# A banded attention with filler products: three Strassen groups in the stage before it, two sets of slots for the turned probabilities, and another order of its steps

## The chip, the cores and the metric

One core of a Trainium2 chip runs the whole kernel in one launch. The metric is the device time of that launch in microseconds (us), as the median of several runs. Engines are named as in the profile: PE is TensorE (PEld its weight load), ACT is ScalarE, DVE is VectorE, POOL is GpSimd, SP is the engine whose queue issues most DMAs.

## What is computed

Two transformer blocks on 1024 tokens of width 1024, all in float32. What matters here is the second block:

```
h = rms_norm(x, norm1_g)
proj = h @ w_in            # 6144 columns: q, k, v (1024 each), bg, cg, xc (1024 each)
q, k = rms_norm per head;  y_attn = chunked_relpos_attention(q, k, v)   # 16 heads of 64
u = cg * xc;  conv = conv_b + sum(conv_w[j] * shifted u);  y_conv = bg * conv
gates = sigmoid(h @ w_gate + b_gate)                                    # 2048 columns
merged = g_attn * (y_attn @ w_attn_proj) + g_conv * (y_conv @ w_conv_proj)
x = x + merged @ w_out;  x = x + square(relu(rms_norm(x) @ w_up)) @ w_down
```

A query of the attention sees the keys of its own chunk of 64 and of the eight chunks before. In tiles of 128 tokens that is a window of at most five key tiles: query tile 0 has one, 1 has two, 2 three, 3 four, and tiles 4 to 7 have five each.

## The kernel before

Every float32 product is made of three matmuls: each operand is split into a high part (rounded to fp32r) and a low part (the rest), and high x high, high x low and low x high are summed in PSUM. Splitting costs ACT or POOL (high) and POOL or DVE (low).

**The stage before the attention** (`phase_qkv`) computes q, k and v, with two "units" of Strassen products (7 products for 8), and then `BCX_GROUPS` more Strassen groups, each for 512 of the 3072 columns bg, cg, xc. A group is 7 products of 24 matmuls (168), where the plain way takes 192. The rest of the 3072 columns, and 7 of the 8 chunks of `w_gate`, are left to be computed as plain "chunks" of 256 columns: a chunk is 4 filler products of 8 steps in k, each step 3 matmuls of 128x512. Only in the last group is the operand of product m6 restored from a copy in DRAM (`spare_x`, loaded by SP at L1897 behind the stores of q and k, L1850; ACT L2091 makes the high part), and the weights of the last product are split behind that on ACT (L2010) and POOL (L1923).

**The attention** (`phase_attention`) goes through 8 pairs of heads, 16 steps a pair, 8 a head; step n of a pair belongs to query tile n % 8. In step n the engines do, in this order (block counts are those of the tile meant):

- PE: half of the step's filler (`product_part`, here 6 matmuls); at odd n the values of the tile pair n-3, n-2 (`values`, L2379, 4 to 12 matmuls); the transposes of the probabilities of tile n-1 (`turn`, L2366); the other half of the filler; the scores of tile n+2 (`scores`, L2354); at n % 8 = 1 and 4 four transposes of raw q and k of the next head (`round_`, L2391). The scores of tile n+2 wait until DVE has read those of tile n+1 (semaphore `shifted`); the turns of tile n-1 wait for its scaled probabilities and for `lo_p`, the low parts of tile n-2.
- ACT: the exponentials of tile n+1 (`exps`, L2517); the eviction of a filler product (`product_out`, L2482) or its store; the high parts of tile n-1 (`high`, L2533); at odd n half of the values' output (`o_tmp`, L2555); at n % 8 = 2 and 5 the high parts of the next head's q and k (`round_hi`, L2466 and L2469, three instructions); v at n % 8 = 3, DMAs at 0 and 7.
- DVE: the bias and the row maximum of tile n+1 (`largest`, L2628); reciprocal and scaling of tile n (L2655, L2656); the low parts of tile n-1 (`low`, L2647); at odd n the sum of the values (L2665); at n % 8 = 3 and 6 the low parts of the next head's q and k (`round_lo`, L2596 and twice L2599); v at 5.
- POOL splits one chunk of filler weights per head (L159, L164); SP loads it.

Every engine works through its list in order; semaphores alone tie the lists. Pairs 1 to 6 run in a hardware loop on PE, ACT and DVE; the first and the last are written out. The high and low parts of turned tiles stand in one set of six slots, so `high` of the next tile pair waits for the values of the one before it.

Of the kernel before, what the change touches and what calls it, by code (L numbers as in the profile page):

```python
# [13 lines left out]
P = 128  # L14
# [40 lines left out]
def program(nc, io, out):  # L55
    ctx = ExitStack()
    with ctx:
# [47 lines left out]
        BCX_GROUPS = 1  # L105
# [2145 lines left out]
        def phase_attention(pairs, src, q_col, k_col, v_col, back, ext, norm_gains, w_start, dst, banks_read, ready_first, ready_rest):  # L2251
# [11 lines left out]
            TAIL = 2 * (STEPS + 2)  # L2263

            def tail_step(x):
                return next(n for n in range(STEPS + 2) if 8 * KB * (2 * n + 2) // TAIL >= KB * (x + 1))
            S_BANK, PT_BANK, O_BANK, G_BANK, T_BANK = 0, 2, 4, 5, 7
            with ExitStack() as mem:
# [9 lines left out]
                pt_hi = sb(mem, "pt_hi_2", [P, nslot, 256], F32R)  # L2278
                pt_lo = sb(mem, "pt_lo_2", [P, nslot, 256], F32R)
# [26 lines left out]
                feed(block, w_start, 2 * pairs + 1, lambda j: (mm_h, j * 4 + 4))  # L2306
# [5 lines left out]
                def pair_loop(eng, body):  # L2312


                    body(0, True, False)
                    with eng.Fori(0, pairs - 2) as j:
                        body(j + 1, False, False)
                    body(pairs - 1, False, True)
# [11 lines left out]
                def pt_groups(m):  # L2330

                    k0, k1 = window(m % 8)
                    sl = k0 - (2 * ((m % 8) // 2) - back)
# [12 lines left out]
                def _(pe):  # L2346
# [23 lines left out]
                    def values(i, m):  # L2370
                        h, g = m % STEPS // 8, (m % 8) // 2
                        pe.wait_ge(lo_p, i * STEPS + (m + 2))

                        pe.wait_ge(o_done, i * 8 + (m // 2 + 1))
                        first, last_kb = window(2 * g)[0], window(2 * g + 1)[1] - 1
                        for kb in range(first, last_kb + 1):
                            sl = kb - (2 * g - back)
# [17 lines left out]
                    def product(chunk, x, ks, out_index):  # L2395
# [3 lines left out]
                        if 0 in ks:  # L2399
                            if x % 4 == 0:  # L2400
                                pe.wait_ge(split_done, chunk + 1)
                            if isinstance(out_index, int) and out_index < 2:
# [13 lines left out]
                    def product_part(i, n, h, last):  # L2416

                        part = 2 * n + h
                        ends = (8 * KB * part // TAIL, 8 * KB * (part + 1) // TAIL) if last else (2 * part, 2 * part + 2)
                        for x in range(ends[0] // KB, (ends[1] - 1) // KB + 1):  # L2420
                            ks = range(max(ends[0] - x * KB, 0), min(ends[1] - x * KB, KB))
                            product(i * 2 + (w_start + 1 + x // 4), x, ks, i * 8 + (EARLY + x))
# [24 lines left out]
                    pair_loop(pe, body)  # L2447

                @block.scalar
                def _(act):  # L2450
# [27 lines left out]
                    def product_out(i, x):  # L2478

                        act.wait_ge(mm_h, i * 8 + (EARLY + x + 1))  # L2480
                        act.wait_ge(st_h[x % 2], (i * 4 + (EARLY + x) // 2 + 1) * 16)
                        nc.scalar.activation(stage[:, x % 2, :], ps[:, G_BANK + x % 2, :], ACT.Copy).then_inc(ev_h, 1)  # L2482

                    def product_store(i, x):

                        act.wait_ge(ev_h, i * 8 + (EARLY + x + 1))
                        act.dma_start(dst[bass.ds(i * (4 * P) + (EARLY + x) // 2 * P, P), (x % 2) * 512:(x % 2 + 1) * 512],
                                      stage[:, x % 2, :]).then_inc(st_h[x % 2], 16)
# [9 lines left out]
                    for r in range(2):  # L2498
                        product_out(0, r - EARLY)
                        product_store(0, r - EARLY)  # L2500
# [4 lines left out]
                    product_out(0, 2 - EARLY)  # L2505
                    product_store(0, 2 - EARLY)
# [14 lines left out]

                    def body(i, first, last):
                        for n in range(STEPS + 2 if last else STEPS):
                            hh, nn = n // 8, n % 8
                            prepare = n < STEPS and not (last and n >= 8)
                            def high():
                                if n <= STEPS and not (first and n < 1):
# [3 lines left out]
                                    act.wait_ge(valued, i * 8 + (m // 2 + 1))  # L2531
# [5 lines left out]

                            if n + 1 < STEPS or not last:
                                exps(i, n + 1)
                            if last and n >= 2:  # L2540
                                for x in range(8):
                                    if n == tail_step(x) + 2:
                                        product_store(i, x)
                                    if n == tail_step(x) + 1:
                                        product_out(i, x)
                            elif n % 2 == 0:
                                product_out(i, n // 2 - 1)
                            else:
                                product_store(i, n // 2 - 1)
                            high()  # L2550
                            if n % 2 and not (first and n < 2):
                                m = n - 2
                                act.wait_ge(valued, i * 8 + (m // 2 + 2))
                                act.wait_ge(o_done, i * 8 + (m // 2 + 1))
                                nc.scalar.activation(o_tmp[:, :], ps[HD:P, O_BANK, 0:256], ACT.Copy).then_inc(o_half, 1)  # L2555
# [14 lines left out]
                    pair_loop(act, body)  # L2570
                    for x in range(8):
                        if tail_step(x) + 1 >= STEPS + 2:
                            product_out(pairs - 1, x)
                        if tail_step(x) + 2 >= STEPS + 2:
                            product_store(pairs - 1, x)

                @block.vector
                def _(dve):
# [5 lines left out]
                    for pt in (pt_hi, pt_lo):  # L2584
                        nc.vector.memset(pt[:, nslot - 1, 0:P].bitcast(F32), 0.0)
                        nc.vector.memset(pt[:, 0, P:256].bitcast(F32), 0.0)
# [47 lines left out]

                    def body(i, first, last):
                        link = Chain(dve, dve_self, i * PER)
                        for n in range(STEPS + 2 if last else STEPS):
# [21 lines left out]
                            if n % 2 and not (first and n < 2):  # L2659
                                m = n - 2  # L2660
                                h, g = m % STEPS // 8, (m % 8) // 2
                                dve.wait_ge(o_half, i * 8 + (m // 2 + 1))
                                pair = i + (m // STEPS)
                                out_rows = res[h * HD:(h + 1) * HD, bass.ds(pair, 1), g * 256:(g + 1) * 256]
                                nc.vector.tensor_tensor(out_rows.rearrange("p a n -> p (a n)"), ps[0:HD, O_BANK, 0:256],  # L2665
                                                        o_tmp[:, :], ALU.add).then_inc(o_done, 1)
# [8 lines left out]
                    pair_loop(dve, body)  # L2675

            products = 8 * pairs + EARLY
            return ([(st_h[s], 16 * (4 * pairs + EARLY // 2 + 1)) for s in range(2)],
# [905 lines left out]
        with nc.Block() as block:  # L3584
# [5 lines left out]
            feat_stored, banks_read = phase_attention(8, qkv2, 0, 1024, 2048, 4, ext2, (io["q_norm_g_2"], io["k_norm_g_2"]), W_BCX2, feat2[512 * BCX_GROUPS:, :],  # L3590
                            banks_read, ready_first, ready_rest)
            opened, banks_read = phase_merge(W_GATE + 5 + 2 * BCX_GROUPS, feat_stored, banks_read)
# [78 lines left out]
```

## Time and profile before

| | us |
|---|---|
| median of 3 runs (2171.71 to 2173.11) | 2171.82 |
| the profiled execution | 2173.93 |
| its span, first to last instruction | 2172.1 |
| PE busy in it | 2145.6 |
| DVE, POOL, ACT busy | 1472.0, 998.3, 949.6 |
| attention steps in it, about | 698 to 1256 |

A matmul's end is modelled in these records, and records overlap; what one costs in a stream is the distance to the next start. Mean granted TensorE clock is 0.998.

### The profile page before, as it was taken

The numbers are of one execution on the slowest core, as the hardware profiler recorded it, in microseconds if no ns is written. First come the engines' busy times: TensorE is split into PE (matmuls) and PEld (weight loads), VectorE is DVE, ScalarE is ACT, GpSimd is POOL, SyncE is SP. The second block draws the span as 40 slices with busy tenths as digits, with TensorE's granted clock in tenths as the row PEclk, the third lists the DMA queues.
The fourth block names the chain that finished last, engine by engine and source line by source line (L and its number), as shares of the span: only waits on it lengthen the run. The fifth ranks groups of instructions, "written<-read, shape, count | busy, mean of one in ns | idle before, by whom it ended". The sixth has DMA issues, their size and how long they took to land.

```text
span 2172.1 us, 29103 instructions
## 1 busy us (share of the span) xinstructions
PE 2145.6 (99%) x10450; PEld 1788.2 (82%) x10450; DVE 1472.0 (68%) x2585; ACT 949.6 (44%) x1696; POOL 998.3 (46%) x701
## 2 busy tenths in 40 slices
PE   8999999999998999999999999999999999999999
PEld 8888888888887888888888888788878887888887
DVE  7776775265874666666666658543776777898886
ACT  5555425343342555555555531212555454433332
POOL 3232465454644131322223147457466565556564
PEclk9999999999999999999999999999999999999999
DMA  7320124332226332323333256315143545826433
GB/s 231 105 76 21 45 91 152 126 117 97 87 88 176 89 108 69 112 72 104 88 93 88 69 195 241 107 49 194 49 154 140 171 146 185 319 93 228 150 122 115
DMA packets 198606, 269.34 MB, mean 124 GB/s; under 512 B 58136, under 2 KB 116280, under 8 KB 198368
## 3 DMA queue, kind: packets, MB, share of 16 engines
q1 hardware_dynamic: 124880, 201.38, 27.5%
q10 hardware_dynamic: 73616, 66.49, 10.0%
q8 instruction: 68, 1.11, 0.2%
q14 instruction: 42, 0.34, 0.1%
HBM read 191.23 MB, written 85.00 MB: 127 GB/s over the span
## 4 chain that ended last, share of the span: by engine, by line
PE 76%; DVE 9%; ACT 5%; DMA 4%; issue 4%; POOL 1%; ACTq 1%; DVEq 0%; SPq 0%; POOLq 0%
PE ps L204 64%; PE ps L2379 3%; DMA w_raw<-in_w_up_dram 2%; PE ps L2354 2%; PE ps L2366 2%; DVE res L3476 1%; DVE mlp_acc L3476 1%; PE ps L776 1%; DMA u_parts<-res 1%; PE ps L751 1%; PE ps L762 1%; DVE k_lo L2599 1%; ACT w_hi L3323 1%; DVE a_lo L446 1%; DVE mlp_acc L3464 1%
## 5 line engine op out<-in xcount | busy, mean ns | idle before, releaser
L204 PE MATMUL ps<-a_hi,w_hi 128*128 128x512 f32 x1376 | 536.9, 407 | 7.4 <-DVE res L2149 5.1
L159 POOL TENSOR_TENSOR w_hi<-w_raw,zero 128x512 fp32r<-128x512 f32 x172 | 203.5, 1214 | 735.6 <-PE ps L204 604.9
L204 PE MATMUL ps<-a_hi,w_lo 128*128 128x512 f32 x1376 | 516.6, 392 | 0.0
L204 PE MATMUL ps<-a_lo,w_hi 128*128 128x512 f32 x1376 | 514.0, 390 | 0.0
L204 PE MATMUL ps<-w_hi,a_hi 128*128 128x512 f32 (+1 forms) x960 | 368.5, 384 | 4.1 <-POOL w_lo L672 2.2
L204 PE MATMUL ps<-w_hi,a_lo 128*128 128x512 f32 (+1 forms) x960 | 367.1, 382 | 0.0
L204 PE MATMUL ps<-w_lo,a_hi 128*128 128x512 f32 (+1 forms) x960 | 366.8, 382 | 0.0
L204 PEld LDWEIGHTS ps<-a_hi,w_lo 128*128 128x128 f32 x1376 | 258.4, 188 | 57.7
L204 PEld LDWEIGHTS ps<-a_hi,w_hi 128*128 128x128 f32 x1376 | 258.8, 188 | 50.8 <-POOL w_lo L1923 5.5
L204 PEld LDWEIGHTS ps<-a_lo,w_hi 128*128 128x128 f32 x1376 | 259.8, 189 | 40.8
L164 POOL TENSOR_TENSOR w_lo<-w_raw,w_hi 128x512 fp32r<-128x512 f32 x172 | 243.4, 1446 | 3.4
L204 PEld LDWEIGHTS ps<-w_hi,a_hi 128*128 128x128 f32 x960 | 180.4, 188 | 40.7 <-POOL w_lo L672 2.4
L204 PEld LDWEIGHTS ps<-w_hi,a_lo 128*128 128x128 f32 x960 | 180.4, 188 | 35.5
L204 PEld LDWEIGHTS ps<-w_lo,a_hi 128*128 128x128 f32 x960 | 180.4, 188 | 35.2
L2647 DVE TENSOR_TENSOR pt_lo<-ps,pt_hi 128x512 fp32r<-128x512 f32 (+1 forms) x192 | 88.3, 488 | 149.0 <-ACT pt_hi L2533 149.0
L2517 ACT ACTIVATE prob<-prob,st 128x640 f32<-128x640 f32 (+4 forms) x128 | 89.4, 698 | 224.5 <-DVE st L2628 223.5
L3237 POOL TENSOR_TENSOR w_lo<-mlp_raw_b,w_hi 128x512 fp32r<-128x512 f32 x60 | 99.0, 1678 | 56.5 <-ACT w_hi L3323 56.5
L3257 POOL TENSOR_TENSOR w_lo<-mlp_raw_more,w_hi 128x512 fp32r<-128x512 f32 x56 | 89.5, 1630 | 62.2 <-ACT w_hi L3354 62.2
L3481 DVE TENSOR_TENSOR a_lo<-mlp_part,a_hi 128x512 fp32r<-128x512 f32 x104 | 108.8, 1094 | 4.8 <-ACT a_hi L3363 4.8
L2628 DVE CUSTOM_DVE_ANT_0 prob<-ps,bias 128x640 f32<-128x640 f32 (+4 forms) x128 | 83.7, 654 | 23.6 <-issue 22.8
L3237 POOL TENSOR_TENSOR w_lo<-w_raw,w_hi 128x512 fp32r<-128x512 f32 x44 | 66.0, 1528 | 63.9 <-ACT w_hi L3323 63.9
L1923 POOL TENSOR_TENSOR w_lo<-qkv_raw,w_hi 128x512 fp32r<-128x512 f32 x46 | 67.2, 1494 | 58.5 <-ACT w_hi L2010 58.5
(307 smaller groups left out, 3929.9 us busy)
## 6 DMA issues: line engine op xcount, KB each, us to landing
mlp_part<-u_parts SPq DMA_DIRECT2D x26, 1024.0 KB, 7.9
w_raw<-in_w_in_dram SPq DMA_DIRECT2D x24, 1024.0 KB, 5.3
feat_fm<-stage ACTq DMA_DIRECT2D x68, 256.0 KB, 2.1
u_parts<-mlp_acc SPq DMA_DIRECT2D x28, 512.0 KB, 2.8
u_parts<-res SPq DMA_DIRECT2D x28, 512.0 KB, 2.8
conv_in<-feat_fm ACTq DMA_DIRECT2D x24, 512.0 KB, 5.5
res<-in_x_dram SPq DMA_DIRECT2D x16, 512.0 KB, 6.4
w_raw<-in_w_out_dram SPq DMA_DIRECT2D x8, 1024.0 KB, 5.1
```

Of the source, the lines that this page charges most:

```text
L159: hi = nc.gpsimd.tensor_tensor(w_hi[slot][:, k:k + 2, :], w_raw[:, k:k + 2, :], zero[:, 0:1].unsqueeze(2).to_broadcast([P, 2, CW]), ALU.add)
L164: lo = nc.gpsimd.tensor_tensor(w_lo[slot][:, k:k + 2, :], w_raw[:, k:k + 2, :], w_hi[slot][:, k:k + 2, :].bitcast(F32), ALU.subtract)
L204: last = nc.tensor.matmul(out_of(o), lhs, rhs(o), start=first and n == 0, stop=final and n == 2)
L1923: ins = nc.gpsimd.tensor_tensor(weight(w_lo, s)[:, at, :], raw_weight(s)[:, at, :], weight(w_hi, s)[:, at, :].bitcast(F32), ALU.subtract)
L2354: last = nc.tensor.matmul(ps[:, S_BANK + bank, 0:c1 - c0], q_st[:, head_slot, b * P:(b + 1) * P], kk[:, head_slot, k0 * P + c0:k0 * P + c1 ...
L2379: last = nc.tensor.matmul(ps[:, O_BANK, 0:256], v_st[:, h, kb, :], pt[:, sl, :], start=(kb == first and pt is pt_hi), stop=(kb == last_kb ...
L2517: nc.scalar.activation(prob[:, s, 0:w], prob[:, s, 0:w], ACT.Exp, scale=-1.0, bias=st[:, s, 1:2], accum_out=st[:, s, 2:3]).then_inc(exped, 1)
L2628: nc.vector.tensor_tensor_reduce(out=tile_view(prob, s, 0, nk), in0=score_view(nk), in1=tile_view(bias, hh, off, nk), scale=-1.0, scalar=3 ...
L2647: ins = nc.vector.tensor_tensor(pt_lo[:, sl:sl + cnt, cols], ps[:, bank, 0:cnt * P].rearrange("p (j n) -> p j n", n=P), pt_hi[:, sl:sl + c ...
L3237: ins = nc.gpsimd.tensor_tensor(low[:, k:k + 2, :], up_raw(p)[:, k:k + 2, :], high[:, k:k + 2, :].bitcast(F32), ALU.subtract)
L3257: ins = nc.gpsimd.tensor_tensor(down_slot(w_lo, s)[:, k, :], raw_of[p][h][:, k, :], down_slot(w_hi, s)[:, k, :].bitcast(F32), ALU.subtract)
L3481: nc.vector.tensor_tensor(down_operand(a_lo, s)[:, k, :], staged(s)[:, k, :], down_operand(a_hi, s)[:, k, :].bitcast(F32), ALU.subtract).t ...
```

## The change

`BCX_GROUPS` goes from 1 to 3, so two more Strassen groups run before the attention and four chunks fewer are filler: 13 instead of 17. The filler is spread evenly over all 130 steps. The loops over pairs are written out. `pt_hi` and `pt_lo` get two sets of slots. On PE the turns come ahead of the second part of the filler and the values last; on ACT `high` comes first, then at even n the half of the values, then `exps`; DVE sums the values at even n, a step later.

```diff
-        BCX_GROUPS = 1
+        BCX_GROUPS = 3
+        FILL_CHUNKS = 13
...
-            TAIL = 2 * (STEPS + 2)
+            FILLED = 4 * (fill_chunks - 1)
+            PARTS = 2 * (STEPS * pairs + 2)
+            def filled_to(part):
+                return FILLED * KB * part // PARTS
+            def last_step(x):
+                return next(n for n in range(PARTS // 2) if filled_to(2 * n + 2) >= KB * (x + 1))
+            OUT_AT = {0: -1, **{last_step(x) + 1: x for x in range(FILLED)}}
+            STORE_AT = {n + 1: x for n, x in OUT_AT.items()}
...
-                pt_hi = sb(mem, "pt_hi_2", [P, nslot, 256], F32R)
-                pt_lo = sb(mem, "pt_lo_2", [P, nslot, 256], F32R)
+                pt_hi = sb(mem, "pt_hi_2", [P, 2 * nslot, 256], F32R)
+                pt_lo = sb(mem, "pt_lo_2", [P, 2 * nslot, 256], F32R)
...
-                feed(block, w_start, 2 * pairs + 1, lambda j: (mm_h, j * 4 + 4))
+                feed(block, w_start, fill_chunks, lambda j: (mm_h, j * 4 + 4))
...
+                    for i in range(pairs):
+                        body(i, i == 0, i == pairs - 1)
...
# PE
-                            product_part(i, n, 0, last)
+                            product_part(i, n, 0)
                             if first and n == 0:
                                 scores(0, 1, 0)
-                            if n % 2 and not (first and n < 2):
-                                values(i, n - 2)
                             if n <= STEPS and not (first and n < 1):
                                 turn(i, n - 1)
-                            product_part(i, n, 1, last)
+                            product_part(i, n, 1)
                             if n + 2 < STEPS or not last:
                                 ...
                                 scores(i, n + 2, (n + 2) // 8 % 2)
+                            if n % 2 and not (first and n < 2):
+                                values(i, n - 2)
# ACT
-                                    act.wait_ge(valued, i * 8 + (m // 2 + 1))
+                                    if i * 8 + m // 2 > 1:
+                                        act.wait_ge(valued, i * 8 + m // 2)
...
+                            high()
+                            if n % 2 == 0 and not (first and n < 4):
+                                out_half(i, n - 3)
                             if n + 1 < STEPS or not last:
                                 exps(i, n + 1)
-                            (store or eviction of a product, by the parity of n)
-                            high()
-                            if n % 2 and not (first and n < 2):
-                                (half of the values of tiles n-3, n-2)
+                            step = STEPS * i + n
+                            if step in STORE_AT:
+                                product_store(STORE_AT[step])
+                            if step in OUT_AT:
+                                product_out(OUT_AT[step])
# DVE
                             low()
-                            if n % 2 and not (first and n < 2):
-                                (sum of the values of tiles n-3, n-2)
+                            if n % 2 == 0 and not (first and n < 4):
+                                out_sum(i, n - 3)
```

## Rows read from the trace of the kernel before

**Rows 1.** The page: busy time, share and instructions of each engine.
```profile
PE 2145.6 (99%) x10450; PEld 1788.2 (82%) x10450; DVE 1472.0 (68%) x2585; ACT 949.6 (44%) x1696; POOL 998.3 (46%) x701
```

**Rows 2.** Waits of PE, 560 to 700 us (us, times, longest).
```profile
PE ps L204 <- DVE res L2149: 5.1, 1, 5.1
```

**Rows 3.** Timeline: start us, length us, engine, line, operation, [idle before <-releaser]; ACT.
```profile
662.22 1.91 ACT L2091 ACTIVATE a_hi<-qkv_spare 128x2048 fp32r<-128x2048 f32 x1 [9.53 <-DMA qkv_spare<-spare_x]
```

**Rows 4.** Timeline of PE behind that wait.
```profile
668.14 0.63 PE L204 MATMUL ps<-a_lo,w_hi 128*128 128x512 f32 x1
...
668.57 0.63 PE L204 MATMUL ps<-a_hi,w_lo 128*128 128x512 f32 x1
```

**Rows 5.** The chain of work: the same values one pair of heads on.
```profile
867.03 1.49 PE ps L2379 x12
...
936.92 1.50 PE ps L2379 x12
```

**Rows 6.** Timeline of PE, attention: steps 3 and 4 of a head.
```profile
1044.91 0.27 PE L2354 MATMUL ps<-k_hi,q_st 128*128 128x256 f32 x1
...
1045.14 0.40 PE L204 MATMUL ps<-a_hi,w_hi 128*128 128x512 f32 x1
...
1059.40 0.28 PE L2379 MATMUL ps<-pt_hi,v_st 128*128 128x256 f32 x1
...
1059.87 0.49 PE L2366 MATMUL ps<-ident,prob 128*128 128x128 f32 x3
...
1061.58 0.45 PE L2354 MATMUL ps<-k_hi,q_st 128*128 128x320 f32 x2
...
1062.16 0.39 PE L204 MATMUL ps<-a_hi,w_hi 128*128 128x512 f32 x1
...
1063.55 0.60 PE L2366 MATMUL ps<-ident,prob 128*128 128x128 f32 x4
...
1065.38 0.45 PE L2354 MATMUL ps<-k_hi,q_st 128*128 128x320 f32 x2
```

**Rows 7.** Timeline of DVE, the same steps and two others.
```profile
1043.83 0.29 DVE L2628 CUSTOM_DVE_ANT_0 prob<-ps,bias 128x128 f32<-128x128 f32 x1
...
1060.99 0.56 DVE L2647 TENSOR_TENSOR pt_lo<-ps,pt_hi 128x384 fp32r<-128x384 f32 x1 [1.35 <-ACT pt_hi L2533]
...
1061.51 0.42 DVE L2665 TENSOR_TENSOR res<-ps,o_tmp 64x256 f32 x1
...
1061.96 0.74 DVE L2596 SCALAR_TENSOR_TENSOR q_st<-ps,gains,q_st 64x512 fp32r<-64x512 f32 x1
...
1064.38 0.82 DVE L2628 CUSTOM_DVE_ANT_0 prob<-ps,bias 128x640 f32<-128x640 f32 x1
...
1070.81 0.89 DVE L2647 TENSOR_TENSOR pt_lo<-ps,pt_hi 128x512 fp32r<-128x512 f32 x2 [1.39 <-ACT pt_hi L2533]
```

**Rows 8.** Timeline of ACT, steps 2, 3 and 5 of a head.
```profile
1054.94 0.73 ACT L2517 ACTIVATE prob<-prob,st 128x512 f32<-128x512 f32 x1 [1.83 <-DVE st L2628]
...
1055.78 0.60 ACT L2482 ACTIVATE stage<-ps 128x512 f32<-128x512 f32 x1
...
1056.28 0.38 ACT L2533 ACTIVATE pt_hi<-ps 128x256 fp32r<-128x256 f32 x1
...
1056.54 0.68 ACT L2466 ACTIVATE q_st<-ps,gains 64x512 fp32r<-64x512 f32 x1
...
1057.23 1.38 ACT L2469 ACTIVATE k_hi<-ps,gains 64x512 fp32r<-64x512 f32 x2
...
1060.47 0.49 ACT L2533 ACTIVATE pt_hi<-ps 128x384 fp32r<-128x384 f32 x1 [0.47 <-PE ps L2366]
...
1070.01 0.77 ACT L2533 ACTIVATE pt_hi<-ps 128x512 fp32r<-128x512 f32 x2 [0.30 <-PE ps L2366]
```

**Rows 9.** Groups of DVE by shape, attention: busy us, mean ns | idle.
```profile
L2656 DVE TENSOR_SCALAR prob<-prob,st 128x640 f32<-128x640 f32 x64 | 35.4, 554 | 2.3
...
L2656 DVE TENSOR_SCALAR prob<-prob,st 128x256 f32<-128x256 f32 x16 | 17.9, 1116 | 0.6
```

More of the change, by code:

```diff
@@ L2249, in phase_qkv, with phase_attention @@
                     [store_q[0, 1].at(32), store_q[1, 1].at(32), b_store[0].at(16 * NG), b_store[1].at(16 * NG)])
-        def phase_attention(pairs, src, q_col, k_col, v_col, back, ext, norm_gains, w_start, dst, banks_read, ready_first, ready_rest):
+        def phase_attention(pairs, src, q_col, k_col, v_col, back, ext, norm_gains, w_start, fill_chunks, dst, banks_read, ready_first, ready_rest):
             nslot = back + 2
@@ L2262, in phase_attention @@
             EARLY = 4
-            TAIL = 2 * (STEPS + 2)
-            def tail_step(x):
-                return next(n for n in range(STEPS + 2) if 8 * KB * (2 * n + 2) // TAIL >= KB * (x + 1))
+            FILLED = 4 * (fill_chunks - 1)
[6 more added lines that the diff above has]
+            STORE_AT = {n + 1: x for n, x in OUT_AT.items()}
+            assert len(OUT_AT) == FILLED + 1
             S_BANK, PT_BANK, O_BANK, G_BANK, T_BANK = 0, 2, 4, 5, 7
@@ L2310, in window, with pair_loop @@
                     return max(0, b - back), b + 1
[L2312 to L2318, printed above, removed]
+                def pair_loop(body):
+                    for i in range(pairs):
+                        body(i, i == 0, i == pairs - 1)
                 def pieces(nk):
@@ L2332, in pt_groups @@
                     k0, k1 = window(m % 8)
-                    sl = k0 - (2 * ((m % 8) // 2) - back)
+                    sl = k0 - (2 * ((m % 8) // 2) - back) + nslot * (m // 2 % 2)
                     cols = slice((m % 2) * P, (m % 2 + 1) * P)
@@ L2376, in values @@
                         for kb in range(first, last_kb + 1):
-                            sl = kb - (2 * g - back)
+                            sl = kb - (2 * g - back) + nslot * (m // 2 % 2)
                             for pt in (pt_hi, pt_lo):
@@ L2401, in product @@
                                 pe.wait_ge(split_done, chunk + 1)
-                            if isinstance(out_index, int) and out_index < 2:
+                            if out_index < 2:
                                 pe.wait_ge(*banks_read[out_index])
@@ L2414, in product, with product_part @@
                             last.then_inc(mm_h, 1)
[L2416 to L2422, printed above, removed]
+                    def product_part(i, n, h):
+                        part = 2 * (STEPS * i + n) + h
+                        begin, end = filled_to(part), filled_to(part + 1)
+                        for x in range(begin // KB, (end + KB - 1) // KB):
+                            ks = range(max(begin - x * KB, 0), min(end - x * KB, KB))
+                            product(w_start + 1 + x // 4, x, ks, EARLY + x)
                     for x in range(EARLY):
@@ L2444, in body @@
                                 scores(i, n + 2, (n + 2) // 8 % 2)
+                            if n % 2 and not (first and n < 2):
+                                values(i, n - 2)
                             if n % 8 in (1, 4) and not (last and n >= 8):
                                 round_(i * 2 + (n // 8 + 1), n % 8 // 4)
[L2447 removed]
+                    pair_loop(body)
                 @block.scalar
@@ L2475, in v_high, with product_out, product_store @@
                         nc.scalar.activation(v_st[:, slot, :, 0:HD], v_raw[:, :, :], ACT.Copy).then_inc(hi_v, 1)
-                    def product_out(i, x):
-                        act.wait_ge(mm_h, i * 8 + (EARLY + x + 1))
-                        act.wait_ge(st_h[x % 2], (i * 4 + (EARLY + x) // 2 + 1) * 16)
+                    def product_out(x):
+                        act.wait_ge(mm_h, EARLY + x + 1)
+                        act.wait_ge(st_h[x % 2], ((EARLY + x) // 2 + 1) * 16)
                         nc.scalar.activation(stage[:, x % 2, :], ps[:, G_BANK + x % 2, :], ACT.Copy).then_inc(ev_h, 1)
[L2484 to L2488, printed above, removed]
+                    def product_store(x):
+                        act.wait_ge(ev_h, EARLY + x + 1)
+                        row = (EARLY + x) // 2 * P
+                        act.dma_start(dst[row:row + P, (x % 2) * 512:(x % 2 + 1) * 512], stage[:, x % 2, :]).then_inc(st_h[x % 2], 16)
                     for ready in ready_first:
@@ L2498, in _ @@
                     for r in range(2):
-                        product_out(0, r - EARLY)
-                        product_store(0, r - EARLY)
+                        product_out(r - EARLY)
+                        product_store(r - EARLY)
                         if r == 0:
@@ L2504, in _ @@
                     nc.scalar.activation(st[:, 3, 3:4], zero[:, 0:1], ACT.Exp)
-                    product_out(0, 2 - EARLY)
-                    product_store(0, 2 - EARLY)
+                    product_out(2 - EARLY)
+                    product_store(2 - EARLY)
                     act.wait_ge(lo_r, 3)
@@ L2520, in _, with out_half @@
                     exps(0, 0)
+                    def out_half(i, m):
+                        act.wait_ge(valued, i * 8 + (m // 2 + 2))
+                        act.wait_ge(o_done, i * 8 + (m // 2 + 1))
+                        nc.scalar.activation(o_tmp[:, :], ps[HD:P, O_BANK, 0:256], ACT.Copy).then_inc(o_half, 1)
                     def body(i, first, last):
@@ L2536, in high @@
                                     ins.then_inc(hi_p, 1)
+                            high()
+                            if n % 2 == 0 and not (first and n < 4):
+                                out_half(i, n - 3)
                             if n + 1 < STEPS or not last:
                                 exps(i, n + 1)
[L2540 to L2549, printed above, removed]
-                            high()
-                            if n % 2 and not (first and n < 2):
[L2552 to L2555, printed above, removed]
+                            step = STEPS * i + n
[3 more added lines that the diff above has]
+                                product_out(OUT_AT[step])
                             if prepare:
@@ L2569, in body @@
                                     load_head(i * 2 + (hh + 2))
[L2570 to L2575, printed above, removed]
+                    pair_loop(body)
+                    out_half(pairs - 1, STEPS - 1)
+                    for x in range(FILLED):
+                        if last_step(x) + 1 >= PARTS // 2:
+                            product_out(x)
+                        if last_step(x) + 2 >= PARTS // 2:
+                            product_store(x)
                 @block.vector
@@ L2584, in _ @@
                     for pt in (pt_hi, pt_lo):
-                        nc.vector.memset(pt[:, nslot - 1, 0:P].bitcast(F32), 0.0)
-                        nc.vector.memset(pt[:, 0, P:256].bitcast(F32), 0.0)
+                        for side in range(2):
+                            nc.vector.memset(pt[:, nslot * side + nslot - 1, 0:P].bitcast(F32), 0.0)
+                            nc.vector.memset(pt[:, nslot * side, P:256].bitcast(F32), 0.0)
                     nc.vector.memset(bias[0:HD, :, wmax - HD:wmax], NEG)
@@ L2633, in _, with out_sum @@
                     largest(0, 0, True)
+                    def out_sum(i, m):
+                        h, g = m % STEPS // 8, (m % 8) // 2
+                        dve.wait_ge(o_half, i * 8 + (m // 2 + 1))
+                        pair = i + (m // STEPS)
+                        out_rows = res[h * HD:(h + 1) * HD, bass.ds(pair, 1), g * 256:(g + 1) * 256]
+                        nc.vector.tensor_tensor(out_rows.rearrange("p a n -> p (a n)"), ps[0:HD, O_BANK, 0:256],
+                                                o_tmp[:, :], ALU.add).then_inc(o_done, 1)
                     def body(i, first, last):
@@ L2658, in body @@
                             low()
-                            if n % 2 and not (first and n < 2):
[L2660 to L2666, printed above, removed]
+                            if n % 2 == 0 and not (first and n < 4):
+                                out_sum(i, n - 3)
                             if n < STEPS and not (last and n >= 8):
@@ L2674, in body @@
                             link.close(PER)
-                    pair_loop(dve, body)
-            products = 8 * pairs + EARLY
-            return ([(st_h[s], 16 * (4 * pairs + EARLY // 2 + 1)) for s in range(2)],
+                    pair_loop(body)
+                    out_sum(pairs - 1, STEPS - 1)
+            products = FILLED + EARLY
+            return ([(st_h[s], 16 * (products // 2 + 1)) for s in range(2)],
                     [[(o_done, 8 * pairs + 1), (ev_h, products - 1)], [(ev_h, products), (lo_r, 4 * pairs + 1)],
```

4 lines of the change are left out of this document (2 added, 2 removed).

## The prediction, made before the changed kernel was run

> **What bounds the kernel now.** I read the page first: PE is busy for 2145.6 of 2172 us [rows 1], so whatever takes matmuls out of its list, or a pause out of it, is worth its full time, and whatever makes it wait costs its full time. The waits view of the stage before the attention has one large pause: 5.1 us, once, in the Strassen group [rows 2]. ACT's timeline names its source: 9.53 us of idle time in front of the high parts of the restored operand, ended by the DMA of `spare_x` [rows 3]; the weights of the last product are split behind it. The matmuls after the pause stand 0.43 us apart [rows 4], those elsewhere 1.39/6 = 0.232 us (rows 6: 1062.16 to 1063.55 is one half of a step's filler).
>
> In the attention the timelines show PE without a gap worth the name, so there its list is the time. One pair of heads takes 936.92 - 867.03 = 69.89 us [rows 5]. What PE itself needs comes from distances of starts [rows 6]: half of the filler (six matmuls) 1.39; transposes of 3 blocks and half a filler 1.71, so 0.32 for 3 blocks, 1.83 - 1.39 = 0.44 for 4, hence 0.56 for 5 and 0.20 for 2; scores of 5 blocks 0.58, of few blocks 0.23; values 0.47 for 4 matmuls. A pair is 32 x 1.39 + 72 values matmuls (8.5) + transposes of two heads (2 x 3.3) + four `round_` (1.8) + scores (7.1) = 68.5. So 1.4 us of a pair are small waits and the loop.
>
> What matters more is how close the other engines are. DVE starts the maximum of tile 5 at 1064.38 and takes 0.82 [rows 7]; the scores of tile 6, which wait for it, start at 1065.38 [rows 6]. That is the release with no slack: PE arrives at just the time at which DVE is done. The chain behind this is (tiles counted from 1): transposes of tile 3 on PE, their high parts on ACT, low parts on DVE, then `round_lo`, 2.42 us from its start to the next maximum (1061.96 to 1064.38), then the maximum, then the scores. Filler on PE is the only thing that covers it.
>
> **The change part by part.**
>
> *Matmuls.* 17 chunks become 13: 4 x 4 x 24 = 384 matmuls go from the attention, 384 x 0.232 = 89.1 us. Two groups of 168 come before it: 336 x 0.232 = 77.9. Net -11.2. DVE, ACT and POOL work of a group (one product takes PE 24 x 0.232 = 5.6 us) fitted in the existing group but for the one pause, so I cost it at nothing; if each added group had a pause like that one, it would be +6.3 each, the upper end.
>
> *The pause of the restored operand.* SP issues the load of `spare_x` behind the stores of q and k, before it turns to the groups, in both kernels; it is needed in the last group. With two groups of 38.9 us in front, a DMA that came 9.5 us late is there long before. I take the whole pause off: 5.1 us and the slow matmuls behind it, six at +0.2: -6.3. The other end is 0, if another release stands right behind; the weights of that product are then split two products ahead, so I see none. The added loads of SP (four of 1 MB, two stored results more) are issued a group ahead of use.
>
> *Old small waits of the attention.* They come from ACT doing the exponentials, which wait for DVE, before the high parts. `high` now goes first, and the second set of slots lets it pass the values. 1.4 x 8 = -11; the other end is 0. Written-out steps instead of a loop: their cost lies within the same 1.4 a pair downward, and as much upward, since other written-out stages run six matmuls in the same 1.39; I take 0. The four added memsets stand in DVE's wait at the start of the stage. ACT has 16 stores and evictions fewer, SP and POOL four chunks fewer: nothing on PE's path.
>
> *Less cover, two places in a head.* A step had 12 filler matmuls; now it has 1152/130 = 8.9, so a half is 1.03 us instead of 1.39. DVE's and ACT's lists are as long as before.
>
> First place, scores of the next head's second tile, in step 7. From the start of the transposes of the sixth tile PE passes: transposes 0.56, half, scores 0.23, half, transposes 0.56, half = 4.43 us (the values, which stood in between, are now behind these scores; before it was 3 x 1.39 + 1.35 + 1.43 for twelve values matmuls = 6.95). The chain that the scores wait for: transposes to high parts 0.60 for 3 blocks (1059.87 to 1060.47), 0.84 for 5; to low parts 0.80 (1070.01 to 1070.81 [rows 7, 8]); low parts 0.89; the sum of the values 0.45, which now falls in just this step, an even one; `round_lo` 2.42; the maximum of one block to the scores 1.00 - (0.82 - 0.29) = 0.47 [rows 7]. Sum 5.87. So PE waits 1.44 us. Before, without the sum, it was 5.42 against 6.95: hidden.
>
> Second place, the scores of the seventh tile, in step 4. PE passes from the transposes of tile 3: 0.32, half, scores 0.58, values 0.47, half, 0.44, half = 4.90. The chain: 0.60 + 0.52 + 0.52 (1060.47, 1060.99, 1061.51) + 2.42 + 1.00 = 5.06, a wait of 0.16. But ACT is late too: it now does, in step 2, the high parts of two blocks (0.26), the half of the values (about 0.4, by DVE's sum of the same tile), the exponentials (0.84), in 37 of 100 steps an eviction (0.50), and `round_hi` (0.69 + 1.38 = 2.07) *after* the transposes of that step, where before the exponentials and the eviction came ahead of them [rows 8]. From the start of those transposes it is free for the next high parts after 0.48 + 0.26 + 0.40 + 0.84 + 2.07 = 4.05, or 4.55; they are ready after 0.20 + 1.03 + 0.58 + 1.03 + 0.60 = 3.44. Late by 0.61 or 1.11, mean 0.80. The wait is 0.96.
>
> Together 2.4 us in each of the 15 heads that prepare a next one: +36. What is behind a PE that waits is all its filler, so none of it comes back. Ends: 0, if the lists slide apart somewhere that I don't see; 15 x 3.4 = +51, if an eviction and a blocked scaling (below) fall in every time.
>
> *Sum* against the profiled execution (2173.93; span 2172.1): -11.2 - 6.3 - 11 + 36 = +7.5, 2181.4. The median of before lies 2.1 under that execution, so 2179 to be compared with 2171.82; I say 2180.
>
> **A rule that speaks against the change.** Scaling 256 columns takes DVE 1116 ns on average, 640 columns only 554 [rows 9]: POOL splits its chunk in the first steps of each head, where the small tiles are, and blocks it there. The Trainium skill ("SBUF — State Buffer", "Who interferes with whom") says that `tensor_scalar` in its two-port mode and GpSimd exclude each other for a whole instruction; this trace agrees, by those two means.
>
> **Rivals.**
>
> 1. *The waits are hidden; PE stays the bound.* Then the time is -28.5: 2143. For it: PE is the bound nearly everywhere now, and DVE has work for two thirds of the time. Against it: the release with no slack at step 4 [rows 6, 7]. It decides if the chain of 5.87 us is shorter by 1.4.
> 2. *Only the place in step 7 waits.* ACT's list is in time after all, so step 4 costs 0.16: 15 x 1.6 = 24, sum -4.5, 2167. For it: ACT is the least loaded. Against: the order of its list.
> 3. *Slower by more, by blocked scalings.* There are 13 splits in 130 steps instead of one at each head's start, so they drift onto five-block tiles, where DVE is the chain. A hit costs up to 1.1 - 0.35 = 0.75 us; one that counts per head is 15 x 0.75 = +11 on the forecast: +19, 2191. It decides once scalings of 640 columns average above 0.75 us. Against it: the scaling stands in front of low parts that are not ready for about 1 us.
> 4. *The added groups bring their own pause* each, +12.6 on the forecast, 2192. Against: what caused the pause is in the last group only.
>
> **Chances.** Forecast (-4 to +17 around +7.5) 0.45, rival 1 0.13, rival 2 0.20, rival 3 0.14, rival 4 0.08. About 0.2% (4.3 us) can be told from no change. Faster by more: rival 1, half of rival 2, a little of the forecast's low end: 0.28. Slower: most of the forecast, rivals 3 and 4: 0.50. Between: 0.22. The likeliest case alone is 2168 to 2189; the range, to hold 8 in 10, is 2151 to 2196.
>
> **What would show it.** In the trace after: scores (L2354) waiting for DVE's maximum (L2628) about 30 times, at some 1 and 1.4 us; a pair of heads in 69.9 - 12 + 5 - 1.4, about 61.5 us, against 56.9 under rival 1; no wait at L2149 or for `qkv_spare`; each added group 38.9 us; DVE's wait for the high parts much smaller. Wrong if a pair takes under 58.5 us: then the two places don't wait; or if PE waits elsewhere, at the transposes or values, for more than 10 us in all.

## The result and the profile after

Six runs of the changed kernel have a median of 2182.36 us (2179.49 to 2183.69), against 2172.26 for the kernel before: ratio 1.0044, 95% interval 1.0033 to 1.0055. It is slower by 10 us; 2180 was forecast, with a range of 2151 to 2196. Lines have moved by 1 to 16 in the changed file: the scores are L2362 (before L2354), the transposes L2374, the values L2387, the transposes of raw q and k L2399, DVE's maximum L2636, `round_lo` L2604 and L2607, the low parts L2663.

The page of the profile after: its span, PE's row, and the first of the chain's shares by line.

```profile
span 2181.6 us, 28219 instructions
...
PE 2134.2 (98%) x10402; PEld 1778.7 (82%) x10402; DVE 1505.6 (69%) x2619; ACT 959.3 (44%) x1714; POOL 1009.5 (46%) x697
...
PE ps L205 73%; PE ps L2387 3%; DVE k_lo L2607 2%; PE ps L2362 2%; PE ps L2374 1%; PE ps L777 1%; DVE q_st L2604 1%; PE ps L752 1%; PE ps L763 1%; DVE prob L2636 1%; DVE pt_lo L2663 1%; DMA v_raw<-qkv_tm 1%; PE ps L2399 1%; DVE a_lo L447 1%; ACT k_hi L2477 1%
```

PE is busy 11.4 us less than in [rows 1], in a span 9.5 us longer. Where that is, the windows view shows, cut at the end of the last Strassen stage and at the end of the last values of the attention (columns: stretch, its length, busy us and instructions of PE, PEld, DVE, ACT, POOL, then clock, DMA share, GB/s). Before:

```profile
628.50:677.60 49.10, 44.04 (x187) 35.85 (x187) 35.53 (x41) 14.54 (x19) 19.65 (x15) 0.97 0.33 113
677.60:1255.80 578.20, 574.92 (x3182) 485.43 (x3182) 369.22 (x1014) 308.47 (x693) 154.63 (x136) 1.00 0.33 93
1255.80:2172.10 916.30, 906.98 (x4006) 746.57 (x4004) 660.16 (x663) 348.96 (x441) 534.15 (x344) 1.00 0.45 157
```

After:

```profile
628.50:748.00 119.50, 119.50 (x525) 98.27 (x524) 65.95 (x72) 36.26 (x54) 59.17 (x43) 1.00 0.32 109
748.00:1268.40 520.40, 490.12 (x2803) 415.25 (x2802) 361.21 (x1017) 295.58 (x677) 122.13 (x104) 1.00 0.32 88
1268.40:2181.60 913.20, 904.83 (x4000) 744.55 (x4000) 671.62 (x663) 350.08 (x441) 538.26 (x344) 1.00 0.45 158
```

The first stretch, from the same start, is 70.4 us longer, the attention 57.8 shorter, the rest 3.1 shorter. In the first stretch the 5 us without PE are gone and the clock is 1.00: two added groups cost 70.4, which is 336 matmuls (77.9) less a pause of some 7.5. `spare_x` is now loaded at 653.38, and ACT's use of it comes at 729.63 without a wait where [rows 3] had 9.53 us:

```profile
653.38 0.51 SPq L1898 DMA_DIRECT2D qkv_spare<-spare_x  x1
```

```profile
729.63 1.90 ACT L2092 ACTIVATE a_hi<-qkv_spare 128x2048 fp32r<-128x2048 f32 x1
```

The waits of PE in the attention (us, times, longest):

```profile
PE ps L2362 <- DVE st L2636: 25.5, 27, 1.3
...
PE ps L2399 <- DMA v_raw<-qkv_tm: 3.4, 2, 2.4
...
PE ps L2374 <- DVE prob L2672: 0.5, 1, 0.5
...
PE ps L2374 <- DVE pt_lo L2663: 0.2, 1, 0.2
```

The first row is the forecast one; the same view of the kernel before has it once, with 0.6 us. The view counts idle time only from the modelled end of the matmul before; measured by the distance of starts less the usual distance (waits above 0.15 us counted), the waits in front of the scores are 30 and sum to 30.8 us, 0.28 to 1.48 each, at two tiles of each head that prepares a next one. Here is one of step 7, three engines:

```profile
852.20 0.71 PE L2374 MATMUL ps<-ident,prob 128*128 128x128 f32 x5
...
856.07 0.40 PE L205 MATMUL ps<-a_hi,w_lo 128*128 128x512 f32 x1
...
857.77 0.38 PE L2362 MATMUL ps<-k_hi,q_st 128*128 128x256 f32 x1 [1.30 <-DVE st L2636]
```

```profile
852.95 0.77 ACT L2547 ACTIVATE pt_hi<-ps 128x512 fp32r<-128x512 f32 x2 [0.64 <-PE ps L2374]
```

```profile
851.97 1.38 DVE L2672 TENSOR_SCALAR prob<-prob,st 128x640 f32<-128x640 f32 x1
853.75 0.89 DVE L2663 TENSOR_TENSOR pt_lo<-ps,pt_hi 128x512 fp32r<-128x512 f32 x2 [0.40 <-ACT pt_hi L2547]
...
854.55 0.41 DVE L2648 TENSOR_TENSOR res<-ps,o_tmp 64x256 f32<-64x256 f32 x1
...
854.99 0.74 DVE L2604 SCALAR_TENSOR_TENSOR q_st<-ps,gains,q_st 64x512 fp32r<-64x512 f32 x1
...
855.75 1.53 DVE L2607 SCALAR_TENSOR_TENSOR k_lo<-ps,gains,k_hi 64x512 fp32r<-64x512 f32 x2
...
857.41 0.29 DVE L2636 CUSTOM_DVE_ANT_0 prob<-ps,bias 128x128 f32<-128x128 f32 x1
```

The transposes of the sixth tile start at 852.20. High parts at 852.95, low parts at 853.75, the sum of the values at 854.55, `round_lo` at 854.99, the maximum at 857.41, the scores at 857.77: the chain is 5.57 us. PE was through with its own list at 856.07 + 0.23 = 856.30, which is 4.10 us after the same transposes, so it waited 1.47. The next pairs of heads:

```profile
931.22 1.44 PE ps L2387 x12
...
992.71 1.42 PE ps L2387 x12
...
1115.07 1.44 PE ps L2387 x12
...
1177.45 1.42 PE ps L2387 x12
```

61.5 and 62.4 us, where [rows 5] had 69.9. All seven such distances lie between 60.7 and 65.9 us, with a mean of 62.3.

### The profile page after: what moved, and what is told of

Same layout as the page of the kernel before. It is cut to its first block, busy times and chain, and to the rows that moved or that the text cites. A ratio compares the mean times of both kernels' runs of the same rounds, so it can differ in the third digit from the quotient of the medians.

```text
span 2181.6 us, 28219 instructions
## 1 busy us (share of the span) xinstructions
PE 2134.2 (98%) x10402; PEld 1778.7 (82%) x10402; DVE 1505.6 (69%) x2619; ACT 959.3 (44%) x1714; POOL 1009.5 (46%) x697
## 4 chain that ended last, share of the span: by engine, by line
PE 83%; DVE 7%; ACT 4%; issue 2%; DMA 2%; POOL 1%; ACTq 0%; DVEq 0%; SPq 0%; POOLq 0%
PE ps L205 73%; PE ps L2387 3%; DVE k_lo L2607 2%; PE ps L2362 2%; PE ps L2374 1%; PE ps L777 1%; DVE q_st L2604 1%; PE ps L752 1%; PE ps L763 1%; DVE prob L2636 1%; DVE pt_lo L2663 1%; DMA v_raw<-qkv_tm 1%; PE ps L2399 1%; DVE a_lo L447 1%; ACT k_hi L2477 1%
## 5 line engine op out<-in xcount | busy, mean ns | idle before, releaser
L160 POOL TENSOR_TENSOR w_hi<-w_raw,zero 128x512 fp32r<-128x512 f32 x156 | 186.8, 1229 | 713.5 <-PE ps L205 596.1
L205 PE MATMUL ps<-a_hi,w_hi 128*128 128x512 f32 x1312 | 511.4, 408 | 3.5 <-DVE a_lo L447 2.1
L205 PE MATMUL ps<-a_hi,w_lo 128*128 128x512 f32 x1312 | 491.2, 392 | 0.0
L205 PE MATMUL ps<-a_lo,w_hi 128*128 128x512 f32 x1312 | 489.2, 391 | 0.0
L205 PEld LDWEIGHTS ps<-a_hi,w_lo 128*128 128x128 f32 x1312 | 246.5, 188 | 54.4
L205 PEld LDWEIGHTS ps<-a_hi,w_hi 128*128 128x128 f32 x1312 | 247.0, 189 | 44.4 <-DVE a_lo L447 4.2
L205 PEld LDWEIGHTS ps<-a_lo,w_hi 128*128 128x128 f32 x1312 | 247.7, 189 | 37.6
L165 POOL TENSOR_TENSOR w_lo<-w_raw,w_hi 128x512 fp32r<-128x512 f32 x156 | 226.0, 1480 | 3.1
L2663 DVE TENSOR_TENSOR pt_lo<-ps,pt_hi 128x512 fp32r<-128x512 f32 (+1 forms) x192 | 87.9, 485 | 110.3 <-ACT pt_hi L2547 110.0
L2547 ACT ACTIVATE pt_hi<-ps 128x512 fp32r<-128x512 f32 (+1 forms) x192 | 77.1, 436 | 174.2 <-PE ps L2374 173.2
L1924 POOL TENSOR_TENSOR w_lo<-qkv_raw,w_hi 128x512 fp32r<-128x512 f32 x66 | 95.9, 1485 | 76.5 <-ACT w_hi L2011 76.5
L3268 POOL TENSOR_TENSOR w_lo<-mlp_raw_more,w_hi 128x512 fp32r<-128x512 f32 x56 | 90.5, 1648 | 60.7 <-ACT w_hi L3365 60.7
L3248 POOL TENSOR_TENSOR w_lo<-w_raw,w_hi 128x512 fp32r<-128x512 f32 x44 | 70.7, 1634 | 47.2 <-ACT w_hi L3334 47.2
```

The costliest lines, as they stand in the source:

```text
L160: hi = nc.gpsimd.tensor_tensor(w_hi[slot][:, k:k + 2, :], w_raw[:, k:k + 2, :], zero[:, 0:1].unsqueeze(2).to_broadcast([P, 2, CW]), ALU.add)
L165: lo = nc.gpsimd.tensor_tensor(w_lo[slot][:, k:k + 2, :], w_raw[:, k:k + 2, :], w_hi[slot][:, k:k + 2, :].bitcast(F32), ALU.subtract)
L205: last = nc.tensor.matmul(out_of(o), lhs, rhs(o), start=first and n == 0, stop=final and n == 2)
L1924: ins = nc.gpsimd.tensor_tensor(weight(w_lo, s)[:, at, :], raw_weight(s)[:, at, :], weight(w_hi, s)[:, at, :].bitcast(F32), ALU.subtract)
L2547: ins = nc.scalar.activation(pt_hi[:, sl:sl + cnt, cols], ps[:, bank, 0:cnt * P].rearrange("p (j n) -> p j n", n=P), ACT.Copy)
L2663: ins = nc.vector.tensor_tensor(pt_lo[:, sl:sl + cnt, cols], ps[:, bank, 0:cnt * P].rearrange("p (j n) -> p j n", n=P), pt_hi[:, sl:sl + c ...
```

## The experiments

Each is timed in rounds beside the kernel before; ratios have 95% intervals. Waits in the attention are summed by distances of starts, as above; they are 38.5 us in the changed kernel, 6.9 before.

**E1. `round_lo` behind the next maximum.** Does the place in the list cost the time, or the amount of work?

```diff
                                 largest(i, n + 1, first and n < 3)
+                            if nn in (4, 7) and n < STEPS and not (last and n >= 8):
+                                round_lo(i * 2 + (hh + 1), (hh + 1) % 2, (nn - 1) // 4)
...
-                                if nn in (3, 6):
-                                    round_lo(head, slot, nn // 4)
```

> VectorE's round_lo stands behind the next tile's maximum (steps 4 and 7 instead of 3 and 6); all else as in the changed kernel. Theory (the scores wait in two places of a head for a maximum that stands behind round_lo): at step 7 the chain falls from 5.87 to about 3.5 us against 4.43 of PE, at step 4 from 5.9 to 3.3 against 4.9, so nearly all of the 30.8 us of waits at the scores go and 0 to 5 come back at the transposes (low parts 2.4 us later): 2150 to 2158 us, and a pair of heads in 57 to 58 us instead of 61.7. Rival A (VectorE simply has too much to do, any order waits): 2178 to 2186, the waits move to the transposes. Rival B (it is ScalarE's lateness): under 10 us gained.

Measured: 2155.61, ratio 0.9926 (0.9914 to 0.9938). Its DVE in step 7, and PE's transposes of the sixth tile and its scores:

```profile
852.17 0.41 DVE L2648 TENSOR_TENSOR res<-ps,o_tmp 64x256 f32<-64x256 f32 x1
...
852.51 0.28 DVE L2636 CUSTOM_DVE_ANT_0 prob<-ps,bias 128x128 f32<-128x128 f32 x1
...
852.83 0.74 DVE L2604 SCALAR_TENSOR_TENSOR q_st<-ps,gains,q_st 64x512 fp32r<-64x512 f32 x1
```

```profile
849.83 0.71 PE L2374 MATMUL ps<-ident,prob 128*128 128x128 f32 x5
...
853.92 0.28 PE L2362 MATMUL ps<-k_hi,q_st 128*128 128x256 f32 x1
```

The maximum now starts 2.68 us after the transposes, not 5.21, and the scores come 4.09 after them, which is PE's own list. A pair of heads takes 57.7 to 59.0 us in the first six distances. No wait in front of the scores is left; 12.7 us remain, 8.4 before transposes, 4.3 before raw transposes, which now wait mostly for `k_lo` (once for the load of v). Same work on the same engine, 27 us less: rival A falls.

**E2. `round_hi` at the head of its steps.**

```diff
+                            if prepare and nn in (2, 5):
+                                round_hi(i * 2 + (hh + 1), (hh + 1) % 2, nn // 4)
                             high()
...
-                                if nn in (2, 5):
-                                    round_hi(head, slot, nn // 4)
```

> ScalarE does round_hi at the head of steps 2 and 5, ahead of the high parts, instead of at their end; all else as in the changed kernel. Theory: only the lateness at step 4 goes (mean 0.80 of 0.96 us in 15 heads, 12 us), the waits at step 7 stay at 0.8 to 1.5: 2169 to 2174 us. Rival A (VectorE has too much to do): no change, 2182. Rival B (ScalarE's lateness is all of it): 2150.

Measured: 2172.17, ratio 1.0000 (0.9991 to 1.0008); waits at the scores 22.4 us instead of 30.8. The waits at step 4 shrank to 0.33 to 0.75 or went away (from 13.3 to 4.5 us in all); those at step 7 stayed at 0.8 and 1.5 (17.9 us in all, before 17.6). ScalarE's lateness is real, 8.4 us of the 30.8; rival B falls.

**E3. The new order with one group** (`BCX_GROUPS = 1`, `FILL_CHUNKS = 17` in the changed kernel).

> The new order, both sets of slots, the written-out steps and the even filler, with one Strassen group and 17 chunks as before. Theory: with 11.8 filler matmuls a step the cover at step 7 is 5.5 against 5.9 us, 0.4 in 15 heads, step 4 is covered; the old small waits of about 7 us at the values go; the pause of 5.1 us at the restored operand stays: 2168 to 2174, within 3 us of the kernel before. Rival C (writing out the steps, or the order, costs by itself): 2178 or more. Rival D (the order is a clear gain): under 2165.

Measured: 2163.78, ratio 0.9963 (0.9950 to 0.9976); one of the six executions took 5536.75 us and is not in the ratio. That is faster than I expected, and by its range it is rival D, a clear gain; E10 asks how much of it is the order's. The 0.4 us a head at step 7 didn't come: the chain is 5.57 us and not the 5.87 of the forecast, PE's list 5.5, and no wait at the scores is left in this trace.

**E4. Three groups with the old order** (all three engines' order and the single set of slots put back; the steps stay written out and the filler even).

> Three groups, 13 chunks, written-out steps and even filler, but the order of the kernel before on PE, ACT and DVE and one set of slots. Theory (a lack of cover, whatever the order): the release at step 4, which had no slack, waits by 3 halves x 0.36 = 1.1 us, and the waits at the values grow by 0.4 to 1 us each: 2 to 3.5 us a head, 2173 to 2195, so about as slow as the changed kernel or slower. Rival E (the new order brings the waits): 2145 to 2155.

Measured: 2210.15, ratio 1.0180 (1.0166 to 1.0194), above my range. PE's waits in the attention:

```profile
PE ps L2387 <- DVE pt_lo L2661: 20.5, 26, 1.4
...
PE ps L2362 <- DVE st L2634: 16.6, 16, 1.7
...
PE ps L2374 <- DVE pt_lo L2661: 9.7, 15, 0.9
PE ps L2399 <- DMA v_raw<-qkv_tm: 3.5, 2, 2.5
```

By distances they are 26.8 us at the values, 19.4 at the scores, 12.7 at the transposes. So the order does not bring the waits: it and the second set of slots together take 28 us off the time; rival E falls. The two were not put back one at a time, so how the 28 us divide between them is open. I had reckoned two places a head; the trace has three kinds. My reading is that the exponentials, which go first in the old order, stand behind the late maximum and make the next low parts late; that link by itself was not tried.

**E5, E6. Both moves, with three and with four groups** (E1 and E2 together; then `BCX_GROUPS = 4`, `FILL_CHUNKS = 11`).

> Both moves, round_lo behind the next maximum and round_hi at the head of its steps, three groups. Theory: the 8.4 us at the transposes and 4.3 us at the transposes of raw q and k (PE now waits there for k_lo) that the first move left shrink by the part that comes from ScalarE's lateness, some 3 us: 2150 to 2155. Rival: ScalarE's lateness is no longer on any path once round_lo is moved: 2155 to 2157, no change against the first move alone.

Measured: 2158.14, ratio 0.9931 (0.9915 to 0.9947): no gain over E1, and so the rival of that expectation (though 1 us above its range) rather than the theory: once `round_lo` is moved, taking ScalarE's lateness away gains nothing that can be told from noise.

> Both moves, four Strassen groups and 11 chunks (7.4 filler matmuls a step). 192 matmuls of filler against 168: 5.6 us less work for PE, and each half of a step is 0.17 us shorter. Theory: the chain of transposes, high parts, low parts of a five-block tile (2.8 us with the release) now stands against 2.7 to 2.9 us of PE in even steps, and the raw transposes wait longer for k_lo: 10 to 25 us of waits more, 2155 to 2172. Rival (cover is still ample): 2146 to 2150.

Measured: 2173.27, ratio 1.0002 (0.9992 to 1.0012). Waits 33.9 us by distances, 26.2 of them at 49 transposes. The view, from modelled ends, names what most of them wait for:

```profile
PE ps L2374 <- DVE pt_lo L2665: 17.0, 40, 1.0
```

The loop from transposes over high and low parts to the next transposes is the bound there. The loss is a little above the range.

**E7. Two groups in the changed kernel** (15 chunks). The order stays, the cover grows.

> The changed kernel as it is, with two groups and 15 chunks (10.3 filler matmuls a step, a half of 1.20 us). Theory: the wait is the missing cover: at step 7 the chain of 5.6 us stands against 1.35 + 3 x 1.20 = 4.95 of PE, 0.65 each, at step 4 5.8 against 5.4: 1.0 us in 15 heads, 15 us; against one group and the same order (2163.8): pause gone 6.3, matmuls 5.6 fewer, waits 15 more: 2164 to 2170. Rival (the third group breaks something that the second does not): 2152 to 2157.

Measured: 2165.45, ratio 0.9964 (0.9952 to 0.9976). Waits at the scores 13.1 us in 19 places, 16 of them 0.75 to 0.78 each. In the same order one group (E3), two and three give 0, 13.1 and 30.8 us.

**E8. The sum of the values behind the maximum of the next step.** One term of the chain.

```diff
                                 largest(i, n + 1, first and n < 3)
+                            if n % 2 and not (first and n < 5):
+                                out_sum(i, n - 4)
...
-                            if n % 2 == 0 and not (first and n < 4):
-                                out_sum(i, n - 3)
```

> VectorE sums the values right behind the maximum of the next odd step, not at the end of the even one; three groups, the rest as in the changed kernel. Theory: the chain at step 7 is shorter by that sum, 0.45 us in each of 15 heads, 6.8 us in all, step 4 unchanged, some 0.1 us back where the values wait for the bank: 2175 to 2178. Rival (a shorter list before round_lo only moves the wait to the transposes): 2182.

Measured: 2178.26, ratio 1.0024 (1.0015 to 1.0033), at the upper end of what was expected. The waits of step 7 went from 1.47 and 0.78 to 1.15 and 0.46, 30.8 to 26.0 in all, with 1.4 back before the values; step 4 is unchanged.

**E9. The first move with two groups.**

> The first move alone (round_lo behind the next maximum), with two groups and 15 chunks. Theory: with three groups 12.7 us of small waits were left in the attention; a half of 1.20 us instead of 1.03 covers most of them, and PE has 5.6 us more of matmuls: 2148 to 2156, about level with three groups (2155.6). Rival (the small waits don't depend on the cover): 2159 to 2162.

Measured: 2150.43, ratio 0.9904 (0.9887 to 0.9920), the fastest of all, 21 us under the kernel before and 32 under the changed one. PE's waits in its attention:

```profile
PE ps L2374 <- DVE pt_lo L2665: 1.2, 3, 0.7
...
PE ps L205 <- DVE res L2648: 0.9, 1, 0.9
...
PE ps L2399 <- DMA v_raw<-qkv_tm: 0.8, 1, 0.8
```

**E10. The kernel before with its loops written out.** E3 had gained 7.6 us; is that the order?

> The kernel before with its loops over pairs written out, nothing else. The new order with one group was 7.6 us faster than the kernel before. Theory (the order takes away the 6.9 us of waits at values, transposes and scores): writing out alone changes nothing, 2170 to 2173. Rival (the gain is the hardware loop's own cost): 2164 to 2167.

Measured: 2166.36, ratio 0.9972 (0.9961 to 0.9983), inside the range of the rival (the gain is the loop's own cost). One pair of heads takes 69.21 us, not 69.89:

```profile
833.91 1.65 PE ps L2377 x12
...
903.12 1.64 PE ps L2377 x12
```

The other distances inside the loop differ by as much (0.6 to 0.8). The waits before the values, which the theory gave to the order, are 2 to 3 us shorter here too. So by the medians most of E3's gain comes with writing out; the order and the slots with one group are worth some 2 to 3 us, and as the two intervals overlap this isn't shown to differ from nothing. They matter clearly only when the cover is thin (28 us in E4 against the changed kernel).

## Why the prediction was right

*Matmuls, -11.2.* The distances are as forecast: PE is busy 11.4 us less.

*The pause, -6.3.* Right, 1.2 too small: 70.4 where 77.9 - 6.3 = 71.6 was forecast. Rival 4 (a pause in each added group) is out.

*Old small waits, -11.* Right in sign, too large: 6.9 us by distances, and part of it was the loop (E10), which I had cost at 0. The 68.5 us for PE's own list of a pair was a sum of rounded distances, and 1.4 was a small difference of large numbers. E3 checks it: with no wait at values or scores its pair takes 68.2 us with 3 filler matmuls (0.7) fewer, so the list is nearer 68.9, and 0.7 of the remaining 1.0 is what E10 took off by writing out.

*Two places, +36.* Right in place, count and cause; a little too large. Measured 30.8: 17.6 at step 7, a mean of 1.17 where 1.44 was forecast, and 13.3 at step 4, a mean of 0.88 where 0.96 was. At step 7 the wait was 1.47 where the three halves held 12 matmuls and 0.78 where they held 15. That 1.47 comes so near 1.44 is luck: the forecast was for an average half, and the chain of 5.57 is 0.3 shorter than the forecast's 5.87. The high parts start 0.75 after the transposes, not 0.84, the low parts let the next instruction in after 0.80, not 0.89, and scores follow a one-block maximum 0.36 after its start, not 0.47. E1 shows the place, E7 the cover, E8 the sum's 0.45 (0.32 of it came back), E2 ScalarE's part: 8.4 us by distances, 12 forecast.

*Nothing else, 0.* Wrong by some 7 us: transposes of raw q and k waited for the next head's loads at two places, and the clock fell once behind that (below). The rest of the kernel came out 3.1 us shorter; before, one wait for split weights of the feed-forward stage was 2.7 us long, with a granted clock of 0.50 for the 3.4 us behind it, and after neither was there:

```profile
1844.77 0.77 PE L204 MATMUL ps<-mlp_op_hi,w_hi 128*128 128x512 f32 x1 [2.74 <-POOL w_lo L3237]
```

Why that wait went away I haven't tested.

Added up: +70.4 - 89.1 + 30.8 - 6.9 + 7 - 3.1 = +9, against 9.5 between the spans. The sum came out nearer than its terms: waits 5 us too large, a pause 1 too small and 3 us gained elsewhere stand against 4 us of old waits that weren't there to gain and 7 us put at nothing, and that they nearly cancel is luck.

*The signs.* The 30 waits and a pair of about 61.5 us came as described; waits of PE at transposes and values stayed far under 10 us. DVE's wait for the high parts became smaller by a quarter (149.0 to 110.0 us in the attention), not "much smaller". The 56.9 us given for a pair under rival 1 should be 69.9 - 12 - 1.4 = 56.5, which changes nothing.

*Rivals.* Rival 1 (hidden) and 2 (step 7 alone) are refuted by the trace: 17.6 us of waits at step 7 and 13.3 at step 4. Rival 3 turned on scalings of 640 columns above 750 ns:

```profile
L2672 DVE TENSOR_SCALAR prob<-prob,st 128x640 f32<-128x640 f32 x64 | 40.4, 631 | 2.3
...
L2672 DVE TENSOR_SCALAR prob<-prob,st 128x256 f32<-128x256 f32 x16 | 7.6, 477 | 0.6
```

631 from 554, and 256 columns down from 1116 to 477 [rows 9]: the slow scalings did drift off the small tiles onto all of them with POOL's splits, but by less than decides. One of 1.38 us stands right in front of the low parts in DVE's rows of step 7 above (851.97); DVE still waited 0.40 us for ACT behind it, so it cost nothing.

## What to carry to other kernels

Filler that is taken out of a list pays in full only as long as the rest still covers the longest chain of the other engines; find the release with no slack before, and add up the chain that ends in it. Work that nobody waits for soon (here the next head's low parts) belongs behind the instruction that the bound engine waits for: moving it was worth 27 us, where the change itself lost 10. Then the amount of filler can be tuned: of the three amounts tried with the move, two groups are fastest, 5 us under three (E9 and E1; their intervals just touch), and with four (E6, both moves) the gain is lost. One group with the move was not tried.

## What was not expected of the hardware

The transposes of raw q and k waited 2.37 us at 869.15 for the load of v of the next head, which landed 9.7 us after its issue (median of its kind 4.9, at most 6.9 before), with a weight load of 1 MB issued 0.4 us after it. Behind that pause the granted clock was 0.50 (1.2 of 2.4 GHz) for 3.4 us, and the matmuls stand 0.43 us apart for about six:

```profile
869.15 0.84 PE L2399 MATMUL ps<-ident,qk_raw 128*128 128x128 f32 x4 [2.37 <-DMA v_raw<-qkv_tm]
...
871.07 0.63 PE L205 MATMUL ps<-a_hi,w_hi 128*128 128x512 f32 x1
...
871.49 0.63 PE L205 MATMUL ps<-a_lo,w_hi 128*128 128x512 f32 x1
```

```profile
869.49:872.90 3.41, 3.41 (x12) 2.73 (x11) 0.00 (x0) 0.00 (x0) 0.00 (x0) 0.50 0.00 0
```

Waits of 1.5 us, of which there were many, were not followed by this, and one at the same place in E4 was not either, though it was as long; there the granted clock stayed at 1.00:

```profile
875.95 0.66 PE L2399 MATMUL ps<-ident,qk_raw 128*128 128x128 f32 x4 [2.51 <-DMA v_raw<-qkv_tm]
```

So here a wait of 2.37 us was followed by the lower clock and one of 2.51 us was not; what decides it is open.

Whether the load was slow because of the weight load was not tried, but the traces of all the kernels point that way: the seven loads of v in the attention that were issued from 1.4 us behind a weight load to 0.8 us ahead of one landed after 8.2 to 9.7 us, all others after at most 8.1, and most of them after 4.3 to 5.5. And a hardware loop of 16 steps cost about 0.68 us a turn (E10), though the waits that went with it are waits for other engines in the trace; what in the loop costs this is open.
